# Masking the diagonal score blocks of a causal attention on VectorE instead of TensorE

## The reference, cut to what matters

```python
def fox_block(q, k, v, cq, ck, q_pos, k_pos):
    s = jnp.einsum('bqhd,bkhd->bhqk', q, k).astype(jnp.float32) * (HEAD_DIM ** -0.5)
    s = s + jnp.swapaxes(cq, 1, 2)[..., :, None] - jnp.swapaxes(ck, 1, 2)[..., None, :]
    mask = k_pos[None, :] <= q_pos[:, None]
    p = jax.nn.softmax(jnp.where(mask, s, -jnp.inf), axis=-1)
    return jnp.einsum('bhqk,bkhd->bqhd', p.astype(v.dtype), v)
```

## Time and profile before

| | us |
|---|---|
| median of 3 runs | 1411.63 |
| lowest and highest run | 1405.93, 1411.88 |
| the profiled execution, its time | 1408.32 |
| the profiled execution, its span | 1406.4 |

### The profile page before, as it was taken

The page is one execution under the profiler, slowest core; times in us unless marked ns, Lnnn a source line. Parts: engine busy times, 40 slices in busy tenths (PEclk is TensorE's granted clock), DMA queues, the critical chain, the costliest instruction groups (busy, mean ns, idle before and its releaser), DMA issues.

```text
span 1406.4 us, 25060 instructions
## 1 busy us (share of the span) xinstructions
PE 1369.0 (97%) x8382; PEld 1086.1 (77%) x8382; DVE 922.0 (66%) x2025; ACT 636.6 (45%) x1364; POOL 575.6 (41%) x606
## 2 busy tenths in 40 slices
PE   8999999999999999999999999999999999999998
PEld 7999767788877777777777777777777777778886
DVE  3789755593376778666433676776776776497775
ACT  6766423332353354445333455555555655422121
POOL 2122442200033234221100556877977867644452
PEclk9999999999999999999999999999999999999999
DMA  7885699987349769787998767448458355556552
GB/s 234 295 281 199 201 268 252 275 273 228 113 139 272 248 223 266 243 266 237 313 321 264 170 189 158 107 98 181 103 109 181 83 114 196 160 169 199 191 177 89
DMA packets 211023, 284.21 MB, mean 202 GB/s; under 512 B 49809, under 2 KB 146481, under 8 KB 207409
## 3 DMA queue, kind: packets, MB, share of 16 engines
q1 hardware_dynamic: 209856, 282.61, 68.7%
q10 hardware_dynamic: 1040, 0.00, 0.0%
HBM read 191.12 MB, written 90.19 MB: 200 GB/s over the span
## 4 chain that ended last, share of the span: by engine, by line
PE 60%; DVE 3%; POOL 2%; ACT 2%; issue 2%; DMA 2%; SPq 1%; DVEq 0%; ACTq 0%; POOLq 0%
PE in_g L927 14%; PE attn_pv L2531 10%; PE attn_s L2601 6%; PE attn_s L2500 6%; PE attn_s L2505 5%; PE attn_pv L2601 5%; PE attn_s L2485 5%; PE attn_s L2513 2%; PE in_b L1102 1%; POOL in_hv L1810 1%; PE in_b L1054 1%; PE attn_s L2554 1%; PE attn_s L2502 1%; PE in_b L1157 1%; PE in_b L1122 1%
## 5 line engine op out<-in xcount | busy, mean ns | idle before, releaser
L927 PE MATMUL in_g<-in_wh,in_xh 128*128 128x512 f32 (+2 forms) x904 | 331.4, 380 | 6.2 <-ACT in_xh L1219 2.4
L927 PE MATMUL in_g<-in_wl,in_xh 128*128 128x512 f32 (+2 forms) x904 | 321.9, 369 | 0.0
L2807 POOL TENSOR_TENSOR attn_probs<-attn_probs,attn_probs_turned 128x512 f32<-128x512 f32 (+3 forms) x200 | 214.3, 1072 | 64.9 <-ACT attn_probs_turned L2633 40.9
L927 PE MATMUL in_g<-in_wh,in_xl 128*128 128x512 f32 (+2 forms) x904 | 236.4, 380 | 1.4 <-DVE in_xl L1532 1.3
L2847 DVE TENSOR_REDUCE attn_tops<-attn_s 128x1 f32<-128x512 f32 (+3 forms) x288 | 159.1, 596 | 108.6 <-PE attn_s L2485 108.6
L2633 ACT ACTIVATE attn_probs_turned<-attn_s 128x512 f32<-128x512 f32 (+1 forms) x352 | 161.2, 545 | 125.7 <-PE attn_s L2505 124.8
L927 PEld LDWEIGHTS in_g<-in_wh,in_xh 128*128 128x128 f32 x904 | 165.5, 189 | 40.8 <-issue 7.4
L927 PEld LDWEIGHTS in_g<-in_wl,in_xh 128*128 128x128 f32 x904 | 165.6, 189 | 27.9
L927 PEld LDWEIGHTS in_g<-in_wh,in_xl 128*128 128x128 f32 x904 | 159.1, 190 | 34.9 <-issue 5.3
L1808 POOL TENSOR_SCALAR in_hs<-in_hs 128x8 f32<-128x8 f32 (+1 forms) x53 | 19.5, 368 | 401.8 <-DVE in_hs L1559 401.8
L2531 PE MATMUL attn_pv<-attn_probs_turned,attn_v 128*64 128x256 f32 (+1 forms) x1216 | 142.1, 363 | 0.0
(11 more groups left out here) (377 smaller groups left out, 2685.8 us busy)
## 6 DMA issues: line engine op xcount, KB each, us to landing
in_xu<-scratch_xt SPq DMA_DIRECT2D x87, 512.0 KB, 5.4
in_xl<-scratch_xt SPq DMA_DIRECT2D x34, 512.0 KB, 4.6
in_raw<-in_w_in SPq DMA_DIRECT2D x40, 256.0 KB, 5.2
scratch_xt<-in_xu SPq DMA_DIRECT2D x19, 512.0 KB, 4.4
scratch_xt<-in_xl SPq DMA_DIRECT2D x17, 512.0 KB, 5.0
scratch_k<-in_x_turned SPq DMA_DIRECT2D x17, 512.0 KB, 7.2
scratch_q<-in_x_turned SPq DMA_DIRECT2D x17, 512.0 KB, 5.4
in_x_turned<-in_x_prompt SPq DMA_DIRECT2D x16, 512.0 KB, 4.8
```

The source lines that it names most:

```text
L927: last = X.matmul(g_ps[b][:, 0:m], x, ws[:, c, w0:w0 + m], start=(c == 0 and h == 0 and ws is wh), stop=(c == KC - 1 and h == 1))
L2807: E.tensor_tensor(acc[:, part:, :], acc[:, part:, :], mine, ALU.add).then_inc(added[engine], 1)
```

## The change

The third product on the diagonal (L2502) goes. In its place VectorE adds a turned mask to the 128 x 128 part of the block in PSUM, in a new step `mask` that stands behind the four scores and ahead of the exponentials, thus ahead of the cycle's maxima on VectorE. The exponential of such a block waits for the mask instead of the score. The turned mask is one more constant (bf16), made by one memset and one affine_select on GpSimd. The planner keeps a count `ahead` of the maxima as before, and in a cycle that holds a diagonal lets `upto` stay one behind it, so that such a cycle has three maxima and the next without a diagonal five. In the last three cycles it doesn't.

```diff
-CONSTS = 8
+CONSTS = 10
...
             G.memset(K.causal[:, :], 0.0).then_inc(s_const, 1)
+            G.memset(K.causal_turned[:, :], 0.0).then_inc(s_const, 1)
...
-            pool.wait_ge(s_const, 5)
+            pool.wait_ge(s_const, 6)
...
+            G.affine_select(out=K.causal_turned[:, :], in_=K.causal_turned[:, :], compare_op=ALU.is_ge, fill=MASKED,
+                            base=0, pattern=[[1, P]], channel_multiplier=-1).then_inc(s_const, 1)
...
-    upto, done = EARLY * HOOKS, {}
+    upto = ahead = EARLY * HOOKS
...
         order += [("scores", b) for b in mine]
+        order += [("mask", b) for b in mine if scores[b][0].kind == "fox" and scores[b][1] >= scores[b][0].first]
         order += [("exp", b) for b in mine]
...
         before = upto
-        upto = min(upto + (LEAD[c] if c < len(LEAD) else CYCLE), len(tops))
+        ahead = min(ahead + (LEAD[c] if c < len(LEAD) else CYCLE), len(tops))
+        upto = max(upto, ahead - any(scores[b][1] >= scores[b][0].first for b in mine if scores[b][0].kind == "fox")) if c < cycles - 3 else ahead
         order += [("top", m) for m in range(before, upto)]
...
                     X.matmul(bank[:, part:, :], y2[h][:, keys], x2[h][:, q], start=True, stop=False)
-                    if u.kind == "fox" and k >= u.first:
-                        X.matmul(bank[:, part, :], causr[:, :], identr[:, :], start=False, stop=False)
...
                     u, k, at = scores[s]
-                    act.wait_ge(s_score, s + 1)
+                    if ("mask", s) in masks:
+                        act.wait_ge(s_masked, masks.index(("mask", s)) + 1)
+                    else:
+                        act.wait_ge(s_score, s + 1)
...
+                if what == "mask":
+                    u, k, at = scores[s]
+                    block = ring_ps[ring.at["scores", s]][:, at, :]
+                    dve.wait_ge(s_score, s + 1)
+                    V.tensor_tensor(block, block, K.causal_turned[:, :], ALU.add).then_inc(s_masked, 1)
...
-        K.ident, K.identb, K.causal = a.sb("ident", [P, P]), a.sb("identb", [P, P], BF16), a.sb("causal", [P, P], BF16)
+        K.ident, K.identb = a.sb("ident", [P, P]), a.sb("identb", [P, P], BF16)
+        K.causal, K.causal_turned = a.sb("causal", [P, P], BF16), a.sb("causal_turned", [P, P], BF16)
```

More of the change, by code:

```diff
@@ L2152, in attention_and_output @@
         s_addp, s_addv, s_den, s_denr, s_rden = (a.sem(k) for k in ("added_p", "added_v", "den", "den_read", "rden"))
+        s_masked, masks = a.sem("masked"), [x for x in order if x[0] == "mask"]
         s_store = [a.sem(f"stored{h}") for h in range(2)]
```

## The result

The changed kernel is slower: a median of 1425.78 us in 4 runs (1422.88 to 1428.49) against 1409.14 in 4 of the kernel before, their quotient 1.0118. The ratio on record, which the tables use, is 1.0135, 95% interval 1.0116 to 1.0154; it fits the median of the kernel before in 15 later runs, 1406.98. The loss is thus some 17 to 19 us. The forecast had the direction of the sum and a third of its size (5.4 us). The profiled execution took 1426.44 us, its span is 1424.2, 17.8 above that of before.

What follows compares the result with a forecast made beforehand. TensorE, busy 97%, was taken to set the pace. Cycles 10, 0, 2, cycle 6 and the moved maxima summed to +0.67 us a head, 5.4 for eight: 1413.7 from the profiled 1408.3, 1417 on the median; range 1402 to 1428.

Steps and rivals of the forecast that it cites:

- The largest term: Cycle 6 of each head: 0.92 us longer, as its exponentials wait for masks from a late VectorE.
- cycles 10, 0 and 2: Diagonal cycles where VectorE idles before its maxima: shorter by 0.26, 0.27 and 0.28 us, with little waiting.
- C: Masks at 0.4 us make ScalarE's row copy hold up cycle 7: 13.8 us lost, 1425 us; chance 0.13.
- D: TensorE's stand in cycle 6 lowers its clock once a head, at least 8 x 1.7 us: 1431; chance 0.04.
- Products removed: 128 mask products leave TensorE: 0.12 us a block, 0.48 a cycle, 15.4 us for 32 cycles.
- The mask: Each of 128 mask additions on VectorE takes 0.29 us from start to semaphore, bounds 0.2 and 0.4.
- the ring: Reused score banks: the third maximum and the entries after it make TensorE wait for exponentials 0, 1 and 2.
- Moved maxima: Cycles 1 and 7 get a 512-column maximum (+0.23 us each), cycle 3 one of 128 (+0.10): +0.56 a head.
- the row that moved there: The row of the next head's unit 0 moves from cycle 7 to 8, ahead of its use: costs nothing.
- The sum: All cycle terms of a head give +0.67 us; times 8 heads, 5.4 us slower.
- A: Only cycle 6 waits; exponentials in cycles 10, 0, 2 come in time: -2.3 us, 1409; chance 0.20.
- B: No wait at all: -15.4 us, 1396; needs VectorE free by about +1.2 in cycle 6; chance 0.13.

Runs made afterwards that it cites:

- e1: The kernel before without the causal mask of the scores: product L2502 left out, no mask on VectorE in its place; ratio 0.9945.
- e4: The changed kernel with cycle 6's blocks masked by TensorE again, the other 96 by VectorE; ratio 1.0032.
- e3: The kernel before with the changed order of maxima alone, its masks still on TensorE; ratio 1.0025.
- e2: The changed kernel without the planner's line for three and five maxima, so the order is as before; ratio 1.0073.
- e7: The changed kernel with four maxima everywhere and cycle 6's blocks masked on TensorE, 96 masks on VectorE; ratio 0.9998 to the kernel before.
- e8: The kernel before with one maximum more in each of cycles 3 and 4 and two in cycle 5, masks on TensorE; ratio 0.9988.
- e9: The changed kernel with four maxima everywhere and VectorE masks in cycles 0 and 10 only, the rest on TensorE; ratio 0.9984.
- e10: The changed kernel with four maxima; the first diagonal block of cycles 0, 2, 10 and all of cycle 6 masked on TensorE; ratio 0.9987.
- e5b: The changed kernel with VectorE's 128 masks replaced by reductions of an SBUF constant that the exponential doesn't wait for, no causal mask; ratio 0.9940.
- e5: The changed kernel with VectorE's 128 masks replaced by additions of two SBUF constants that the exponential doesn't wait for, no causal mask; ratio 1.0071.

## Why the prediction was right or wrong

The largest term was right in size and mechanism, the direction of the sum too. What failed is the term of cycles 10, 0 and 2, and the price of nothing that the sum gave to the clock. That 1425.78 lies within the stated 1402 to 1428 is luck: the upper part was there for the better half of rivals C and D, and C's mechanism didn't come.

- **Products removed, 0.12 a block.** Nearly right as a distance (0.58 against 0.69, over four blocks 0.42 and not 0.48), wrong as a gain: the text counted it whole, 15.4 us, then took waits off. Alone it is 7.8. The estimate from the Trainium skill (TensorE: Matmul & The Clock Gate, Back-to-back issue gap), 10.4 us for 128 products of about 81 ns, is above the measured gain as well; e1 gives no price of a product, since TensorE isn't the limit all the way.
- **The mask, 0.29.** Measured 0.289.
- **Cycle 6, +0.92.** Measured +0.87, by the waits that were named: the exponential behind VectorE behind cycle 5's dens, then the ring. VectorE was there at +1.91, not +2.09; a first wait of 0.20 for the den wasn't foreseen, and of the two waits for exponentials the view names one, 0.65. e4 confirms it: it was the largest part of the loss.
- **Cycles 10, 0, 2, -0.81 together.** This is the step that failed in the steady cycles: measured -0.24, which is 0.57 a head or 4.6 us. Two causes. "VectorE is free at +0.72" was read from the kernel before, while the same text put a fifth maximum into cycle 1 ahead of it; it is free at +1.06. With the masks at +0.77 cycle 2 would be 1.10 + 3.35 = 4.45, close to the forecast's 4.41, so this accounts for nearly all of its 0.30. In cycles 0 and 10 the first exponential starts about when forecast (+1.11, and between +1.1 and +1.4 by head), and the cycles are 0.09 and 0.16 longer than reckoned: the slack that the text saw between the chain and TensorE wasn't there.
- **Moved maxima, +0.56.** Right for cycles 1, 3 and 7 (+0.50). Not seen: +0.08 in cycle 8, which is the row that moved there and was put at nothing, and cycle 9, which cost 1.0 in two heads (e3 has it with the masks on TensorE, so it is the order's, together with slow sums on VectorE). "VectorE idles there before its maxima" was true of cycle 7 and not asked of 8 and 9. Together these are 0.08 x 8 + 2.1, under 3 us.
- **The clock, rival D at 0.04.** In part it came: some 5.1 us of the profiled execution behind cycle 6, as large a miss as that of cycles 10, 0 and 2. D had it in every head, 13.6 us; it was three of eight. The reading of the earlier trace rows, that a cycle with such a stand keeps its clock, holds for head 2 (4.95 us, busy 4.10, clock 1.00) and fails for head 3 (busy 5.37 of 6.22, clock 0.78) with the same gaps. From cycles 6 and 7 of all eight heads, one profiled execution each: the changed kernel has a lower clock in three, e2, which has the same wait, in two (0.85 in both), and e3, e4, e7 and e8, without the wait, in none. So the stand in cycle 6 makes it possible and not certain. The statement of the Trainium skill (Perfetto Trace Analysis, Matmul Optimizations), that power follows utilisation and wants products back to back, agrees with this side. The low clock at the start of head 0 is another matter: e4, e2 and e8 have it (0.78, 0.77, 0.77 over its first two cycles), and e8 has no mask on VectorE; e3 has 1.00. Why it comes in some executions isn't settled; each kernel has one trace, so it can't be told whether it goes by the kernel at all. No run tried to fill the stand in cycle 6 with work, so that the stand brings the low clock is borne out by 5 of 16 such cycles against none of 32, and not by a test.
- **The sum, by these parts.** 5.4 + 4.6 (cycles 10, 0, 2) + 2.7 (cycles 8 and 9) + 5.1 (clock) - 0.9 (cycle 6 and the moved maxima a little cheaper than forecast) = 16.9, where the medians are 16.6 apart and the ratio says 19.
- **A, B, C.** B needed VectorE free by +1.2 in cycle 6; even then, as e7 shows, the gain is nothing to speak of, not 15.4. C's row copies ended in time.

e9 and e10, with 48 and 72 masks on VectorE, are lowest at 0.9984 and 0.9987. Their intervals end at 0.9998, just below 1, but e8, whose heads are as long as before, reads 0.9988 as well, so a gain of 0.1 or 0.2% isn't shown. Leaving the mask out gives 0.9945 and 0.9940 (e1 and e5b).

## What to carry to other kernels

Before counting what leaves the busiest engine, ask what is next behind it, here a chain of exponentials and banks 0.30 us away: what lies on that chain costs its full latency, however idle its engine is on average. Read when an engine is free from a schedule in which the other parts of the change are already in place, and follow moved work two cycles on, to the next thing that waits for its engine. A stand of about a microsecond on TensorE can be followed by a lower clock that costs more than it does (1.7 us here, in 5 of 16 cases); since the clock differs from one execution to the next, compare it before a difference of two profiles is put down to a change.

## What was not expected of the hardware

An addition on VectorE with both inputs and the output in SBUF, 128 columns, took 0.275 to 2.012 us in e5 (1.36 in the row shown, where GpSimd was in additions of its own from 901.79 to 905.86), while the masks, which read and write PSUM and take one input from SBUF, stayed between 0.275 and 0.300 in the changed kernel, also the 53 of 128 that lay for the most part beside an addition of GpSimd. In e5 the 99 that lay so took 0.545 in the median, the other 29 0.285. The kernel's own sums on VectorE show it too: 1.71 us for 512 columns in e3 in cycle 9, where the kernel before has 1.07, and 0.68 in head 3 of the changed kernel. A reduction of one SBUF input stayed at 0.268 to 0.288 in e5b. That GpSimd's additions are the cause is read from the timelines; no run took them away.
